# A gated transformer block and two sparse-attention layers: sliding-window attention between the projections, compression weights in a buffer of their own, later splits

## The chip, the cores and the metric

The kernel runs on one core of a Trainium2 chip. The metric is the device time in microseconds (us) of one launch. All tensors are float32 in memory.

## What is computed

The sequence has 256 tokens (T) and 1024 features (D, eight chunks of 128, C = 8). The first block, cut to what matters here:

```python
mod = silu(c) @ w_ada + b_ada                      # 6 x 1024 values, "modulation"
shift1, scale1, gate1, shift2, scale2, gate2 = split(mod, 6)
h = norm1(x) * (1 + scale1) + shift1
q_g, k_g, v_g, a_lr, r_g, q_s, k_s, v_s = split(h @ w_in)
log_a = log_sigmoid(a_lr @ w_gla_alpha + b) / 16
o_gla = rms_norm(gla_mixer(q_g, k_g, v_g, log_a)) * silu(r_g)  # 4 heads, chunks of 64 tokens
o_swa = rms_norm(swa_mixer(q_s, k_s, v_s, sinks))              # 8 heads of 64, softmax with a sink
x = x + gate1 * (concatenate([o_gla, o_swa]) @ w_out)
h2 = norm2(x) * (1 + scale2) + shift2
x = x + gate2 * peer_mixer(h2)                     # top 16 of 128 + 128 keys, 8 heads, 16384 experts
```

Then come a layer with DSA attention (an indexer picks 64 keys per query, 8 heads over a shared latent) and an MLP of 4096; the shared keys and values, of which two are compressed, `gelu(flat(blocks) @ w1) @ w2`, with a `w1` of 4096 x 256 for keys (w1k) and one for values (w1v); a layer with NSA attention and an MLP; and a last norm.

## The kernel before, in words

**Weights.** SyncE (SP) brings 488 blocks of 128 x 1024 floats (512 KB each) in one fixed order into `ring`, which has 4 places (RING). A load waits until the block four places ahead of it has been used (`slots_used`). Where a product needs more than one pass of precision, ScalarE (ACT) writes a rounded copy `ring_hi` (2 places, `split_high`, L368) and VectorE (DVE), or GpSimd (POOL) for `peer_q` and `peer_u`, writes the rest in place as `ring_lo` (`split_low`, L375). TensorE (PE) then does three matmuls for each 128 x 128 tile (`three`, L587 to L589): 24 for a block. The w_in projections use float32 matmuls straight from `ring`: `project` (L555) and `project_tokens` (L567), 16 records a block for `project`.

**Modulation.** The 48 rows of w_ada (512 KB each) are loaded by POOL's queue. The first 16 (shift1 and scale1) have places of their own; the other 32 pass through `aring`, 4 places, each load waiting in POOL's program (L444) until the row 4 ahead is used. `modulation` (L1638) multiplies and sums one row on DVE.

**Order of the first block.** (1) Modulation rows 0 to 5; the bias table waits for all six small loads (`small_loaded`, L1646); the norm of x is a sum over partitions with `ones` on PE (L577), a root on ACT, a reciprocal of 128 x 256 on DVE (L1649); then rows 6 to 15, each pair with one chunk of h. (2) 18 projections in the order q_g, k_g, r_g, q_s, k_s, v_g, v_s. Beside them DVE prepares the decays and rows 16 to 33. (3) The exponentials of the decays on ACT (L1288 to L1292), products on DVE (L1690 to L1695), then GLA on PE: scores (L755), transposes (L762), states (L771), inner part (L780), part between chunks (L788). (4) The norm of GLA: sums (L794, L795), roots, the reciprocal of 128 x 1024 (L1730), scaling (L1732), gate (L1736), splits of the result. (5) Sliding-window attention (`attend("swa")`): 16 units of one head and 128 queries, the first 8 with 128 keys, the others with 256; a unit has scores (L666), transposes (L675) and products (L702) on PE, bias, maximum and scaling on DVE, the exponential and copies on ACT. Rows 40 to 47 lie between its units. (6) Its norm. (7) w_out, 8 blocks; each yields one chunk of x, added by DVE (L1818). (8) The sum of squares of x (POOL adds chunks, L455, L458), norm 2, h2 chunk by chunk (L1804, L1810). (9) peer_q: 16 blocks, low parts by POOL; after each, DVE picks the best 16 keys (L1843 to L1853). (10) peer_u, 128 blocks.

**Memory.** `big` has 128 rows of 256 floats. In the first block it holds h, `aring`, silu(c) (`cs`, rows 37 to 40), projections and GLA's tensors. For the experts rows 40 to 127 must be set to one: POOL does this in three parts, `mid_lo` to `mid_hi` (rows 61 or 62 to 96) after GLA is done (L449), and the other two after the last split of the attention results (L451, L452). `ones_set` is awaited by DVE before the expert gates.

**Later layers.** Before `attend("dsa")` and `attend("nsa")`, ACT and DVE split the first block of a_o and the first two of b_o. In the compression w1k (8 blocks) and w1v (8 blocks) come through the ring one after the other (L1075 to L1077), 12 matmuls a block.

## Time and profile before

| | us |
|---|---|
| median of 3 runs (1765.46 to 1768.02) | 1766.5 |
| the profiled execution's own time | 1767.21 |
| its span, first to last instruction | 1765.6 |
| PE busy in the span | 1650.5 (93%) |
| DVE busy | 1078.7 (61%) |
| ACT busy | 855.1 (48%) |
| POOL busy | 487.9 (28%) |
| mean clock granted to TensorE | 0.951 of full |

The span leaves 1.6 us of the profiled execution outside it. Times of a stage below are counted from the span's start. PE's busy time says how long it had work, not how fast it did it: the granted clock of a stretch says that.

### The profile page before, as it was taken

How to read it: one execution, taken by the hardware profiler on the slowest of the kernel's cores; microseconds unless marked ns; L12 is line 12 of the kernel's file. 1: busy time of each engine (PE TensorE's matmuls, PEld its weight loads, DVE VectorE, ACT ScalarE, POOL GpSimd, SP SyncE). 2: the span in 40 equal slices, each digit the busy share in tenths (PEclk: the TensorE clock that was granted, in tenths of full speed). 3: DMA queues.
4: the chain of work that ended last, by engine and by line, in shares of the span. 5: the costliest groups of instructions: out<-in, count | busy, mean ns of one | idle time of the engine just before them, and what ended most of it. 6: DMA issues, size and time to landing. Idle time of an engine off the chain costs nothing.

```text
span 1765.6 us, 33664 instructions
## 1 busy us (share of the span) xinstructions
PE 1650.5 (93%) x11072; PEld 1492.8 (85%) x11072; DVE 1078.7 (61%) x2455; ACT 855.1 (48%) x1808; POOL 487.9 (28%) x465
## 2 busy tenths in 40 slices
PE   5975889998999999999999999889999998899998
PEld 2773689998999999987888887779999988789997
DVE  5536558953777771355555555866555665755555
ACT  3213445555454444555555554265555535654554
POOL 3110456986666668500000001320000000310000
PEclk8985699999999999999999999889999999999999
DMA  8861144554443445555555555215555456045554
GB/s 309 312 226 57 39 138 144 170 178 140 143 140 134 142 143 169 182 192 192 192 190 190 190 190 178 78 58 165 181 181 185 147 176 205 25 144 175 185 187 155
DMA packets 81329, 288.17 MB, mean 163 GB/s; under 512 B 10144, under 2 KB 11472, under 8 KB 81136
## 3 DMA queue, kind: packets, MB, share of 16 engines
q1 hardware_dynamic: 72448, 257.30, 44.6%
q0 software_dynamic: 7488, 26.87, 4.1%
q10 hardware_dynamic: 1328, 3.15, 0.5%
q8 instruction: 39, 0.64, 0.1%
q14 instruction: 26, 0.21, 0.0%
HBM read 284.66 MB, written 2.62 MB: 163 GB/s over the span
## 4 chain that ended last, share of the span: by engine, by line
PE 83%; DVE 8%; ACT 3%; issue 2%; DMA 2%; POOL 1%; SPq 0%; DVEq 0%; ACTq 0%; POOLq 0%
PE pu L587 12%; PE pu L588 12%; PE pu L589 12%; PE pacc L646 8%; PE pacc L644 8%; PE pacc L645 8%; PE pu L555 3%; PE pu L567 2%; PE pacc L587 2%; PE pacc L589 2%; PE pacc L588 2%; PE pacc L702 2%; PE pm L874 2%; PE pn L874 2%; DVE ring_lo L375 1%
## 5 line engine op out<-in xcount | busy, mean ns | idle before, releaser
L368 ACT ACTIVATE ring_hi<-ring 128x512 fp32r<-128x512 f32 x912 | 524.2, 622 | 546.7 <-PE pu L589 290.5
L375 DVE TENSOR_TENSOR ring_lo<-ring,ring_hi 128x512 fp32r<-128x512 f32 x624 | 407.4, 695 | 356.5 <-ACT ring_hi L368 356.1
L587 PE MATMUL pu<-Xh,ring_hi 128*128 128x256 f32 x1472 | 432.5, 294 | 21.6 <-DVE stats L1756 4.3
L588 PE MATMUL pu<-Xl,ring_hi 128*128 128x256 f32 x1472 | 420.1, 285 | 0.0
L589 PE MATMUL pu<-Xh,ring_lo 128*128 128x256 f32 x1472 | 420.0, 285 | 0.0
L375 POOL TENSOR_TENSOR ring_lo<-ring,ring_hi 128x512 fp32r<-128x512 f32 x288 | 370.3, 1307 | 131.4 <-ACT ring_hi L368 130.8
L587 PEld LDWEIGHTS pu<-Xh,ring_hi 128*128 128x128 f32 x1472 | 285.9, 194 | 28.8 <-issue 15.7
L588 PEld LDWEIGHTS pu<-Xl,ring_hi 128*128 128x128 f32 x1472 | 286.5, 195 | 0.2
L589 PEld LDWEIGHTS pu<-Xh,ring_lo 128*128 128x128 f32 x1472 | 285.8, 194 | 0.0
L644 PE MATMUL pacc<-ring_hi,vh 128*128 128x512 f32 x512 | 200.5, 392 | 0.0
L646 PE MATMUL pacc<-ring_lo,vh 128*128 128x512 f32 x512 | 200.5, 392 | 0.0
L645 PE MATMUL pacc<-ring_hi,vl 128*128 128x512 f32 x512 | 199.8, 390 | 0.0
L587 PE MATMUL pu<-X2h,ring_hi 128*128 128x256 f32 x512 | 146.3, 286 | 3.2 <-DVE big L2088 3.2
L589 PE MATMUL pu<-X2h,ring_lo 128*128 128x256 f32 x512 | 145.6, 284 | 0.0
L588 PE MATMUL pu<-X2l,ring_hi 128*128 128x256 f32 x512 | 145.6, 284 | 0.0
L644 PEld LDWEIGHTS pacc<-ring_hi,vh 128*128 128x128 f32 x512 | 96.0, 187 | 33.2 <-issue 5.6
L646 PEld LDWEIGHTS pacc<-ring_lo,vh 128*128 128x128 f32 x512 | 96.1, 188 | 21.0
L645 PEld LDWEIGHTS pacc<-ring_hi,vl 128*128 128x128 f32 x512 | 96.2, 188 | 16.0
L473 POOL DMA_DIRECT2D big<-bias_row x8 | 4.3, 549 | 363.1 <-DVE stats L1999 363.1
L587 PEld LDWEIGHTS pu<-X2h,ring_hi 128*128 128x128 f32 x512 | 99.0, 193 | 4.2 <-DVE big L2088 3.6
L588 PEld LDWEIGHTS pu<-X2l,ring_hi 128*128 128x128 f32 x512 | 98.9, 193 | 0.3
L589 PEld LDWEIGHTS pu<-X2h,ring_lo 128*128 128x128 f32 x512 | 99.0, 193 | 0.0
(390 smaller groups left out, 2653.1 us busy)
## 6 DMA issues: line engine op xcount, KB each, us to landing
ring<-in_weights SPq DMA_DIRECT2D x488, 512.0 KB, 3.3
big<-in_ada POOLq DMA_DIRECT2D x40, 512.0 KB, 6.7
bias_row<-big ACTq DMA_DIRECT2D x1, 1536.0 KB, 6.9
XT<-in_xT ACTq DMA_DIRECT2D x1, 1024.0 KB, 8.2
scr<-in_ada POOLq DMA_DIRECT2D x2, 512.0 KB, 12.3
tk<-in_ada POOLq DMA_DIRECT2D x2, 512.0 KB, 14.0
early_h<-in_ada POOLq DMA_DIRECT2D x2, 512.0 KB, 16.0
early_l<-in_ada POOLq DMA_DIRECT2D x2, 512.0 KB, 17.6
```

What stands on the lines that cost most here:

```text
L368: nc.scalar.activation(ring_hi[:, n % 2, half], ring[:, n % RING, half], ACT.Copy).then_inc(s["split_hi"], 1)
L375: api.tensor_tensor(ring_lo[:, n % RING, half], ring[:, n % RING, half], ring_hi[:, n % 2, half], ALU.subtract).then_inc(s[LOW[name][0]], 1)
L555: last = mm(entry(e), slot(n)[:, c * P:(c + 1) * P], rhs[:, c, :], start=(c == 0), stop=(c == C - 1))
L567: last = mm(entry(e)[:, tt * P:(tt + 1) * P], lhs[:, c, tt * P:(tt + 1) * P], slot(n)[:, c * P:(c + 1) * P], start=(c == 0), stop=(c == C ...
L587: mm(out, ring_hi[:, n % 2, w], xh, start=start, stop=False, skip_group_check=True)
L588: mm(out, ring_hi[:, n % 2, w], xl, start=False, stop=False, skip_group_check=True)
L589: return mm(out, ring_lo[:, n % RING, w], xh, start=False, stop=stop, skip_group_check=True)
L644: mm(out, xh[:, rows], ring_hi[:, n % 2, w], start=False, stop=False, skip_group_check=True)
L645: mm(out, xl[:, rows], ring_hi[:, n % 2, w], start=False, stop=False, skip_group_check=True)
L646: last = mm(out, xh[:, rows], ring_lo[:, n % RING, w], start=False, stop=False, skip_group_check=True)
L702: last = mm(out, v, p, start=(kind != "nsa" and k == 0 and UNITS[u][4]), stop=(k == len(pairs) - 1 and UNITS[u][5]), skip_group_check=(kin ...
L874: last = mm((pm, pn)[k % 2][:, i * P:(i + 1) * P], sq[:, j // 2, j % 2 * P:(j % 2 + 1) * P], scr[:, j * P:(j + 1) * P], start=True, stop=True)
```

## The change

First block. w_in is laid out as q_s, k_s, v_s, q_g, k_g, v_g, r_g. The 20 steps of the sliding-window attention are spread over the 12 projections from the seventh on (one or two after each, in the programs of PE and ACT), with scores in two PSUM banks (pm, pn) where they had four. ACT computes the decays' exponentials after the sixth projection; DVE's products for GLA and one modulation row are fillers between attention units. r_g is stored as it is, and its SiLU is taken once later. The three norms (n1, swa, gla) sum with tokens on partitions (a product with one column of ones), take the root and the reciprocal of a few columns, and spread them back by a matmul of a broadcast column with the identity; the scaling reads PSUM. w_out is laid out in 8 blocks of half the inputs and a quarter of the outputs: 4 blocks for the attention's half of the inputs, then 4 for GLA's. Each block adds into two chunks of x, so x is added to twice. Rows 40 to 43 of the modulation lie between these blocks, rows 44 to 47 behind h2. The bias table waits for its own two loads only. The first 16 rows of w_ada have six semaphores where they had eight (rows 8 to 11 and 12 to 15 are awaited as four). POOL's two last parts of setting ones are cut into 14 pieces, one behind each of the first 14 peer_q blocks; before the first peer_q split POOL waits until all 48 modulation rows are used. POOL's h2 sum leaves out one chunk more, which PE adds.

Later layers. w1k leaves the ring (480 blocks are left): POOL's queue loads its 4 MB into places of its own after the squares of the first MLP's input are summed, and its splits read from there. The first split of a_o, and the first two of b_o, are done between attention units.

The diff, cut:

```diff
-            for dst, src, sem in ((cols[:, :], cols_d, "cols_loaded"), (relb[0:NB, :], relb_d, "small_loaded"),
-                                  (oneh[0:NB, :], onehot_d, "small_loaded"), (walr, small_d[:, :, 0:16], "small_loaded"),
+            for dst, src, sem in ((cols[:, :], cols_d, "cols_loaded"), (relb[0:NB, :], relb_d, "relb_loaded"),
+                                  (oneh[0:NB, :], onehot_d, "relb_loaded"), (walr, small_d[:, :, 0:16], "small_loaded"),
...
             pool.wait_ge(s["gla_done"], 1)
             for k in range(mid_lo, mid_hi, 4):
                 step(nc.gpsimd.memset(big[:, k:min(k + 4, mid_hi), :], 1.0))
-            pool.wait_ge(s["x_split"], 2 * XSPLIT["w_out"] + 2)
-            step(nc.gpsimd.memset(big[:, GATED_FROM:mid_lo, :], 1.0))
-            nc.gpsimd.memset(big[:, mid_hi:NKEY, :], 1.0).then_inc(s["ones_set"], 1)
             pool.wait_ge(s["h2_sq"], 2)
             h2sum = R[:, T:2 * T]
             step(nc.gpsimd.tensor_tensor(h2sum, sq[:, 0, :], sq[:, 1, :], ALU.add))
-            for c in range(2, C - 1):
+            for c in range(2, C - 2):
                 pool.wait_ge(s["h2_sq"], c + 1)
                 last = nc.gpsimd.tensor_tensor(h2sum, h2sum, sq[:, c, :], ALU.add)
-                if c < C - 2:
+                if c < C - 3:
                     step(last)
             last.then_inc(s["h2_sum"], 1)
             pool.wait_ge(s["slots_used"], SLOT["peer_q"])
+            pool.wait_ge(s["x_split"], 2 * XSPLIT["w_out"] + 2)
+            pool.wait_ge(s["ada_used"], MOD)
+            parts = [(k, min(k + 4, hi)) for lo, hi in ((GATED_FROM, mid_lo), (mid_hi, NKEY)) for k in range(lo, hi, 4)]
             for i in range(2 * PH):
                 split_low(pool, nc.gpsimd, "peer_q", i)
+                for lo, hi in parts[i::2 * PH]:
+                    step(nc.gpsimd.memset(big[:, lo:hi, :], 1.0))
+            nc.gpsimd.memset(ones_flag, 1.0).then_inc(s["ones_set"], 1)
...
+            pool.wait_ge(s["slots_used"], SLOT["a_o"])
+            for k in range(8):
+                pool.dma_start(w1_raw[k], w1k_d[k, :, :]).then_inc(s["w1_full"], 16)
...
                 def scores(u):
-                    if u >= 4:
-                        pe.wait_ge(s["att_biased"], u - 3)
-                    mm(score_psum(u)[:, 0:keys_of(u)], query(u), keys(u), start=True, stop=True)\
+                    if u >= banks:
+                        pe.wait_ge(s["att_biased"], u + 1 - banks)
+                    mm(score_psum(u, banks)[:, 0:keys_of(u)], query(u), keys(u), start=True, stop=True)\
                         .then_inc(s["att_scored"], 1)
...
-            norm_sum("n1")
-            pe.wait_ge(s["small_loaded"], 16 * 6)
+            pe.wait_ge(s["squares"], SQUARED["n1"])
+            for tt in range(TT):
+                for c in range(C):
+                    last = mm(pn[:, tt:tt + 1], sq[:, c, tt * P:(tt + 1) * P], ones[:, 0:1], start=(c == 0), stop=(c == C - 1))
+            last.then_inc(s["sums"], 1)
+            pe.wait_ge(s["consts_made"], 1)
+            pe.wait_ge(s["inverses"], 1)
+            for tt in range(TT):
+                last = mm(pm[:, tt * P:(tt + 1) * P], over_columns(R[:, tt:tt + 1]), ident[:, :], start=True, stop=True)
+            last.then_inc(s["spreads"], 1)
+            pe.wait_ge(s["relb_loaded"], 16 * 2)
...
+            for i in range(18):
+                if i == 5 or 10 <= i < 14:
+                    project_tokens(SLOT["w_in"] + i, USE["w_in"] + i, HTf)
+                else:
+                    project(SLOT["w_in"] + i, USE["w_in"] + i, HTf)
...
+                if i == EARLY:
+                    pe.wait_ge(s["la_parts"], 1)
+                    pe.wait_ge(s["evacs"], USE["w_in"] + EARLY)
+                if i >= EARLY:
+                    for step in steps_after(i - EARLY, swa_steps):
+                        swa_step(SPAN["swa"][0] + step)
...
+            def out_slot(i):
+
+                n, e, x0 = SLOT["w_out"] + i, USE["w_out"] + i, i // 4 * 4
+                pe.wait_ge(s["evacs"], e - 1)
+                if i % 4 == 0:
+                    pe.wait_ge(s["x_split"], 2 * XSPLIT["w_out"] + i // 4 + 1)
+                for j in range(2):
+                    for c in range(4):
+                        if j == 0 and c % 2 == 0:
+                            split_ready("w_out", i, c // 2, None)
+                        last = three(pu[:, e % 2, j * T:(j + 1) * T], n, slice(c * T + j * P, c * T + (j + 1) * P),
+                                     Xh[:, x0 + c, :], Xl[:, x0 + c, :], c == 0, c == 3)
+                last.then_inc(s["slots_used"], 1)
...
+            out_slot(0)
             pe.wait_ge(s["squares"], SQUARED["gla"])
...
+            for h in range(GH):
+                for tt in range(TT):
+                    last = mm(paccf[:, h * TT + tt:h * TT + tt + 1], sq[:, h, tt * P:(tt + 1) * P], ones[:, 0:1], start=True, stop=True)
+            last.then_inc(s["sums"], 1)
+            out_slot(1)
+            pe.wait_ge(s["inverses"], 3)
+            for h in range(GH):
+                for tt in range(TT):
+                    col = 8 + h * TT + tt
+                    last = mm((pm, pn)[h // 2][:, (h % 2 * TT + tt) * P:(h % 2 * TT + tt + 1) * P], over_columns(R[:, col:col + 1]),
+                              ident[:, :], start=True, stop=True)
+            last.then_inc(s["spreads"], 1)
+            for i in range(2, 8):
+                out_slot(i)
...
-                    n = SLOT[name] + i
+                    n = SLOT["w1v"] + i
+                    high, low = ring_hi[:, n % 2, :], (ring_lo[:, n % RING, :] if kv else w1_lo[i][:, :])
...
+                        mm(out, xh, high[:, w], start=(i == 0 and l == 0), stop=False, skip_group_check=True)
+                        mm(out, xh, low[:, w], start=False, stop=False, skip_group_check=True)
+                        last = mm(out, xl, high[:, w], start=False, stop=(i == 7 and l == 3), skip_group_check=True)
+                    last.then_inc(s["slots_used" if kv else "w1_used"], 1)
...
+                if i == EARLY - 1:
+                    act.wait_ge(s["ex_ready"], 1)
...
+                    f(kp, kp, ACT.Exp, scale=inv).then_inc(s["ex_done"], 1)
+                    act.wait_ge(s["row_stored"], 16)
+                if i >= EARLY:
+                    for st in steps_after(i - EARLY, swa_steps):
+                        swa_step(SPAN["swa"][0] + st)
+            swa_step(SPAN["swa"][1] + 4)
+            act.wait_ge(s["att_out"], OUTNO[SPAN["swa"][1] - 1] + 1)
+            squares(os_, sq[:, 0:4, :])
...
+            split_high(act, "w_out", 0)
...
+            split_high(act, "w_out", 1)
+            act.wait_ge(s["evacs"], USE["w_in"] + 18)
+            f(rs, rs, ACT.Silu).then_inc(s["silu_done"], 1)
+            act.wait_ge(s["normed"], NORM["swa"])
+            x_high(os_, 0)
...
+            def dsa_between(i):
+
+                if i == 10:
+                    split_high(act, "a_o", 0)
+
+            attend("dsa", lambda u: (slice(0, P), oT[:, UNITS[u][2], UNITS[u][1] * P:(UNITS[u][1] + 1) * P]), dsa_between)
...
+            def w1k_high(i):
+
+                act.wait_ge(s["w1_full"], 16 * 8)
+                if i >= 2:
+                    act.wait_ge(s["w1_used"], i - 1)
+                for half in halves:
+                    f(ring_hi[:, (SLOT["w1v"] + i) % 2, half], w1_raw[i][:, half], ACT.Copy).then_inc(s["split_hi"], 1)
+
+            w1k_high(0)
...
+                if i == 10 or i == 12:
+                    split_high(act, "b_o", i // 2 - 5)
...
+            modulation(2 * C, 6)
...
+            def swa_filler(i):
+
+                modulation(2 * C + 6 + i, 1)
+                if 8 <= i < 8 + 3 + NSUB:
+                    gla_product(i - 8)
+
+            dve.wait_ge(s["consts_made"], 1)
+            dve.wait_ge(s["small_loaded"], 16 * 4)
+            attend("swa", swa_bias, filler=swa_filler)
+            modulation(2 * C + 23, 1)
...
+            dve.wait_ge(s["spreads"], 2)
+            for i in range(4):
+                last = v.scalar_tensor_tensor(os_[:, i, :], os_[:, i, :], column("swa_g", i), paccf[:, 0:T], ALU.mult, ALU.mult)
+            last.then_inc(s["normed"], 1)
+            split_low(dve, v, "w_out", 0)
...
-            step(v.reciprocal(Rg, Rg))
+            v.reciprocal(R[:, 8:8 + GH * TT], R[:, 8:8 + GH * TT]).then_inc(s["inverses"], 1)
+
+            def out_residual(i):
+
+                e = USE["w_out"] + i
+                dve.wait_ge(s["slots_used"], SLOT["w_out"] + i + 1)
+                for j in range(2):
+                    o = 2 * (i % 4) + j
+                    last = v.scalar_tensor_tensor(XT[:, o, :], pu[:, e % 2, j * T:(j + 1) * T], mod[:, 16 + o:17 + o], XT[:, o, :],
+                                                  ALU.mult, ALU.add)
+                last.then_inc(s["evacs"], 1)
+
+            out_residual(0)
+            modulation(2 * C + 25, 1)
+            dve.wait_ge(s["spreads"], 3)
...
+            dve.wait_ge(s["silu_done"], 1)
             v.tensor_tensor(og, og, rs, ALU.mult).then_inc(s["gla_done"], 1)
...
+            split_low(dve, v, "w_out", 2)
+            out_residual(1)
+            x_low("w_out", og, 1)
+            for i in range(2, C):
+                if i + 1 < C:
+                    split_low(dve, v, "w_out", i + 1)
+                out_residual(i)
+                if i < 4:
+                    modulation(2 * C + 24 + i, 1)
+            rest = 2 * C + 28
...
+            modulation(rest, MOD - rest)
+            dve.wait_ge(s["ada_used"], MOD)
+            step(v.tensor_tensor(mod[:, 40:48], mod[:, 40:48], cols[:, COL["b_ada"] + 40:COL["b_ada"] + 48], ALU.add))
...
+            def dsa_filler(i):
+
+                if i == 12:
+                    split_low(dve, v, "a_o", 0)
+
+            attend("dsa", dsa_bias, filler=dsa_filler)
...
+            def w1k_low(i):
+
+                for j, half in enumerate(halves):
+                    dve.wait_ge(s["split_hi"], 2 * (SPLIT["w1k"] + i) + j + 1)
+                    v.tensor_tensor(w1_lo[i][:, half], w1_raw[i][:, half], ring_hi[:, (SLOT["w1v"] + i) % 2, half], ALU.subtract)\
+                        .then_inc(s["split_lo"], 1)
+
...
+                elif i == 12 or i == 14:
+                    split_low(dve, v, "b_o", i // 2 - 6)
                 elif i == 23:
                     x_low("b_o", oT[:, 0:4, :], 0)
...
+    def halves_of(w):
+
+        return w.reshape(4, P, 4, T).transpose(2, 1, 0, 3).reshape(4, P, D)
...
+        tiles(np.concatenate([qs, ks, vs, qg, kg, vg, rg], axis=1)), halves_of(w_out[512:]), halves_of(w_out[:512]),
```

## Rows read from the trace of the kernel before

**Rows 1.** Busy time by stage: from:to, length, each engine's busy us (instructions), clock, DMA share, GB/s.

```profile
42.00:112.40 70.40, 67.65 (x373) 60.12 (x372) 28.75 (x46) 13.33 (x27) 9.52 (x18) 0.95 0.83 309
112.40:140.30 27.90, 17.49 (x212) 16.53 (x212) 13.69 (x27) 6.92 (x10) 3.17 (x6) 0.59 0.40 133
140.30:161.90 21.60, 5.01 (x12) 2.11 (x12) 14.15 (x15) 8.02 (x10) 0.00 (x0) 0.50 0.00 0
161.90:197.60 35.70, 32.83 (x96) 17.19 (x96) 29.05 (x98) 16.66 (x64) 10.34 (x13) 0.52 0.18 60
197.60:206.80 9.20, 3.49 (x9) 2.30 (x9) 3.58 (x6) 3.09 (x5) 0.00 (x0) 0.78 0.00 0
206.80:233.10 26.30, 26.30 (x194) 26.07 (x194) 12.54 (x21) 11.73 (x22) 16.14 (x8) 0.88 0.45 140
233.10:244.90 11.80, 6.34 (x26) 4.87 (x24) 9.21 (x20) 5.89 (x12) 4.93 (x4) 0.71 0.15 49
244.90:298.40 53.50, 51.11 (x427) 50.72 (x427) 38.04 (x223) 27.07 (x64) 36.93 (x30) 1.00 0.47 158
```

**Rows 2.** The waits of PE: who for whom, us in total, times, longest.

```profile
PE pm L755 <- DVE big L1695: 9.7, 1, 9.7
```

**Rows 3.** DVE's instructions in order of time at the start.

```profile
22.60 0.68 DVE L1647 COPY big<-big 32x1024 f32<-32x1024 f32 x1 [3.23 <-DMA sinks<-in_sinks]
23.21 1.73 DVE L1649 RECIPROCAL R<-R 128x256 f32<-128x256 f32 x1
```

**Rows 4.** One modulation row on DVE: min/median/max ns.

```profile
L1638 DVE CUSTOM_DVE_ANT_0 big<-big x40: 1204/1224/1409, 11.7 to 191.8; 128x1024 f32<-128x1024 f32 x40
```

**Rows 5.** The chain that ended last, in attention: 1.2 GHz at 184, 2.4 GHz at 1520.

```profile
184.84 0.62 PE pacc L675 x2
185.46 1.05 PE pacc L702 x4
186.50 1.15 PE pu L666 x2
...
1520.51 0.45 PE pacc L702 x4
1520.95 0.43 PE pn L666 x2
1521.39 0.11 PE pacc L675
```

**Rows 6.** Stages by clock: inside the projections, and the first of w_out.

```profile
52.50:59.40 6.90, 6.17 (x15) 4.96 (x16) 6.44 (x10) 0.86 (x3) 0.00 (x0) 0.51 0.37 117
59.40:112.40 53.00, 52.96 (x323) 48.59 (x321) 22.30 (x37) 7.03 (x17) 9.52 (x18) 1.00 0.88 327
206.80:213.00 6.20, 6.20 (x29) 6.20 (x30) 1.23 (x1) 1.65 (x3) 3.79 (x1) 0.50 0.00 0
```

**Rows 7.** POOL's groups, 160 to 235 us: busy us, mean ns, idle before.

```profile
L449 POOL MEMSET big<- 128x1024 f32 (+1 forms) x9 | 8.2, 915 | 0.5
L458 POOL TENSOR_TENSOR R<-R,sq 128x256 f32<-128x256 f32 x5 | 3.7, 739 | 7.2 <-ACT sq L1168 7.1
```

**Rows 8.** POOL's group in the peer_q stage, 244.9 to 296 us.

```profile
L375 POOL TENSOR_TENSOR ring_lo<-ring,ring_hi 128x512 fp32r<-128x512 f32 x28 | 35.6, 1293 | 17.9 <-ACT ring_hi L368 17.9
```

**Rows 9.** Groups in the compression, 1444 to 1476 us.

```profile
L375 DVE TENSOR_TENSOR ring_lo<-ring,ring_hi 128x512 fp32r<-128x512 f32 x30 | 19.3, 686 | 13.5 <-ACT ring_hi L368 13.2
L368 ACT ACTIVATE ring_hi<-ring 128x512 fp32r<-128x512 f32 x31 | 17.9, 623 | 15.0 <-DMA ring<-in_weights 9.3 <-PE pm L1077 4.8 <-PE pn L1077 0.8
```

**Rows 10.** DVE in order of time, before NSA's and DSA's first units.

```profile
1504.48 2.50 DVE L375 TENSOR_TENSOR ring_lo<-ring,ring_hi 128x512 fp32r<-128x512 f32 x4 [5.52 <-ACT ring_hi L368]
1506.90 0.28 DVE L2218 TENSOR_TENSOR big<-pm,big 128x128 f32<-128x128 f32 x1
...
1148.78 1.83 DVE L375 TENSOR_TENSOR ring_lo<-ring,ring_hi 128x512 fp32r<-128x512 f32 x2
1150.54 0.28 DVE L2071 TENSOR_TENSOR big<-pm,big 128x128 f32<-128x128 f32 x1
```

315 lines of the change are left out of this document (161 added, 154 removed).

## The prediction

> **What bounds the kernel now.** The page comes first: TensorE is busy for 93% of the span, so only stages with a slow or waiting PE can give much. The stage table shows where they are: from 112.4 to 206.8 us the granted clock is 0.50 to 0.59 of full, 0.78 in the last 9.2 us, and PE has 5.0 us of work in the 21.6 us of GLA's norm [rows 1]. The waits put one idle stretch of 9.7 us on DVE's last GLA product [rows 2]. The chain of waits then tells which engine each stage hangs on. The start hangs on DVE: 3.23 us for the last small load, then 0.6 and 1.7 us before the scaling [rows 3]. The projections hang on PE (67.7 of 70.4 us), attention on PE at 1.2 GHz (32.8 of 35.7), peer_q on PE (51.1 of 53.5) with POOL behind it at 36.9 [rows 1]. All times below are in the profiled execution, 1767.2 us, which is 0.7 above the median of 1766.5.
>
> **The start.** The bias table no longer waits for six loads (3.2 us of idle DVE), its copy (0.6) moves before row 0, and the reciprocal of 256 columns (1.7) becomes one of two: 5.5 us off DVE's line [rows 3]. Rows 4 and 5 are used after the reciprocal, when DVE would have waited. The new sum is 16 products with one column, 32 records. No such product is in the trace; bounds are a 128-column record at 2.4 GHz, 0.11 us, and at 1.2 GHz, 0.31 [rows 5], so 3.5 to 9.9 us against 5.3 us of room between the squares (11.7) and the end of row 3 (about 17). I take 0.13 each, nearer to the first, and 0.5 us of loss: minus 5.0 (minus 1 to minus 5.6). Projections then start at 37.1.
>
> **Attention between the projections.** Removed: 35.7 us [rows 1]. Added on PE: at 2.4 GHz a unit of 256 keys is 0.43 + 2 x 0.11 + 0.45 = 1.10 us, one of 128 keys half; at 1.2 GHz it is 0.62 + 1.05 + 1.15 = 2.82 [rows 5]. PE is kept busy, so I take the first: 8 x 1.10 + 8 x 0.55 = 13.2 us. Where two steps follow each other the product waits for ACT's copy, 0.3 us eight times, and the last unit's chain is open, 0.9: 16.5 together (13.2 to 32.8, today's busy time). DVE: today's 29.1 us less eight modulation rows of 1.3 (1.22 and a readout of 0.08) [rows 1, 4] leave 18.7; seventeen rows are 22.1 and GLA's products 4.4, so 45 us. They lie beside 11 projections of 3.5 us and 16.5, 55 us: covered, with 10 to spare. Projections end at 37.1 + 70.4 + 16.5 = 124.0, and the exponentials and products (9.7, rows 2) are under them.
>
> **GLA and w_out.** GLA's own steps are latencies in a stage of small matmuls at 0.59 [rows 1]: 18.2 us (27.9 less 9.7), kept as they are. Added: attention's norm, 8 one-column products (16 records, 2.0; 1.8 to 5.0) and two spreads (0.9): 145.1. Then ACT's queue decides: copies 1.2, one split 1.2, a table load and SiLU 2.3, the rounded copy of attention 1.1, and DVE's remainder 1.2, of which 3.3 us outlast the last GLA product: w_out starts at 148.4. A block is 24 matmuls, 5.1 us at 1.2 GHz (6.20 / 29 = 0.214 each) [rows 6] and 2.9 at full clock (51.1 / 427 = 0.12) [rows 1]. Block 0 at the low clock 5.1; GLA's sums 2.5; block 1 half and half 4.0; eight spreads 2.2; DVE then scales (1.7), gates (1.2) and splits block 2: PE waits 3.7; block 2 slow again 5.1; five blocks at 2.9 and small waits 14.9. Sum 37.5, against 26.3 now (30 to 43), end 185.9. GLA's norm (21.6) and attention's (9.2) are hidden or inside this sum. Against 233.1: minus 47.2.
>
> **To h2.** The last block adds and squares two chunks (plus 0.8). POOL is passed too: it issues the loads of rows 40 to 47 only when their places free, the last after row 43, which I put at 177 on DVE, so its first nine memsets (8.2 us) [rows 7], free now, end at 186, and five additions of 0.74 follow, 190, where PE wants the sum at 188: plus 2.4 (0 to 5). h2 is ready at 185.9 + 11.8 [rows 1] + 3.2 = 200.9, minus 44.0.
>
> **peer_q: the cost.** Today POOL has split the first two blocks before h2 is ready, and 16 blocks and the hand-over take 53.5 us from there [rows 1]. Now POOL waits for row 48, and DVE does rows 44 to 47 behind h2: 4 x 1.22 + 0.1 = 5.0 us. Nothing hides this, PE's first matmul waits for that split. Then POOL needs 35.6 / 14 = 2.54 us a block [rows 8] and 14 memsets of about 0.95 and a semaphore, 1.0 [rows 7]. PE's block is 3.3 us, POOL's now 3.54: POOL becomes the bound. 5.0 + 16 x 2.54 + 14 x 1.0 + PE's last half 1.5 + hand-over 3.7 = 64.8: plus 11.3 (5 if the memsets slip in, 14 if PE's clock falls in the longer idle). DVE's picks are not pushed: DVE idles there today until PE's first scores. Expert blocks start 32.7 us earlier, and nothing after them depends on more than that.
>
> **Compression.** ACT waits 9.3 us for ring loads there, DVE has 19.3 + 3 us of work in 32 us [rows 9]. With w1k at hand the ring refills behind it. A block is then held by the two places of ring_hi, a split half (0.62) and a remainder half (0.69) after block n-2, 1.5 us a block: I estimate 26.5 us, 5.0 to gain from 31.5 (2 to 8). The 4 MB are loaded in the first MLP, where the DMA engines are half free; 0.3 us for that (0 to 3).
>
> **Later splits.** NSA: DVE's first unit comes 2.5 us after the split begins [rows 10]; moved between units the splits cost 2 x 1.3 on DVE and 2 x 1.2 on ACT, both with some idle: minus 1.7 (minus 2.9 to plus 1). DSA: the split of 1.83 us before the first unit [rows 10] returns among units that run at DVE's pace: 0 (minus 1 to plus 1).
>
> In that row two halves take 0.92 us each, where four before NSA take 0.63 each: POOL adds its bias at the time [rows 10]. The Trainium skill (SBUF — State Buffer, Who interferes with whom) says that a DVE instruction with two SBUF inputs contends with a GpSimd instruction that reads SBUF. By that rule the moved a_o split stays at 1.83 and holds POOL's bias, and DSA's sum would be plus 0.7 rather than 0.
>
> **Sum.** -5.0 - 35.7 + 16.5 - 9.7 + 2.9 + 3.3 - 21.6 - 9.2 + 11.2 = -47.3 (47.2 by the clock times); +3.2; +11.3; -5.0; +0.3; -1.7 = -39.1. 1767.2 - 39.1 = 1728.1; less 0.7 gives 1727.4, forecast 1728.
>
> **Rivals.** (a) POOL's hand-over is free: the memsets fit PE's gaps and PE makes up the wait. Minus 13.7: 1714. For it: POOL idles 17.9 us in peer_q [rows 8]; against: that idle time is before its first split too, and the wait for row 48 stands in its program.
>
> (b) DVE sets the pace of the new order. If it gives a unit 1 us later than PE needs, 16 units are 16 us, and w_out's blocks with a modulation row between them (3.4 us of DVE against 2.9) add 4: 1748. For it: 45 of 55 us, in order, with a wait for ACT in each unit.
>
> (c) Slower than before: PE's clock. After the 2.7 us of waiting at 50.5, the next 6.9 us ran at 0.51 and held 15 records, one projection; at full clock 323 records, 160 of them in the five token blocks of 32 and 163 in blocks of 16, are 15.2 blocks in 53.0 us, 3.5 each [rows 6]. If waits for attention keep PE at 1.2 GHz, twelve projections cost 3.4 us more each, 41, and attention today's 32.8 in place of 16.5, 16: 1785. It passes the kernel before once eight of the twelve run so (8 x 4.8 = 38.4). Against: each projection is 3.5 us of unbroken work between the steps.
>
> The Trainium skill (TensorE: Matmul & The Clock Gate, HAM oscillation) warns that a loop which idles between short bursts of matmuls falls back to half clock each time. By that rule (c) is what happens; this trace shows it after one gap only.
>
> (d) The later layers' edits do nothing, as their waits are replaced by the next: plus 6.4, 1734, inside the forecast.
>
> **Chances.** The forecast with (d), 1720 to 1738: 0.57. (a), below 1720: 0.16. (b), 1738 to 1760: 0.21. (c) or any other loss: 0.05; no change 0.01. A measurement can tell 0.2% (3.5 us). Faster 0.94, same 0.01, slower 0.05. The range, 1712 to 1748, takes in (a) and most of (b); the unit costs alone (attention 13 to 33, w_out 30 to 43) span as much.
>
> **What would show it.** Projections from 37 to 124 us at a clock of 0.95 or more; no 128 x 1024 reciprocal; w_out in some 37 us with one wait of 3 to 4; POOL's first peer_q split after the 48th modulation row, and PE waiting for POOL in most peer_q blocks; ACT's wait for ring loads in the compression near 0. Projections at half clock, DVE as the releaser of PE between projections, or peer_q at 54 us would prove it wrong.

## The result, and the profile after

| | before | after |
|---|---|---|
| median of the runs taken together (4 each), us | 1766.3 | 1734.18 |
| lowest to highest, us | 1765.46 to 1768.02 | 1732.42 to 1737.05 |
| span of the profiled execution, us | 1765.6 | 1730.7 |
| mean clock granted to TensorE | 0.951 | 0.974 |

The two medians are 32.1 us apart. The ratio on record is 0.9833, with an interval of 0.9816 to 0.985, and 1.67% of 1766 us is 29.5 us. The kernel before was at the upper end of its scatter in this set: in the three later sets its medians were 1761.5, 1762.1 and 1764.4 us, and the changed kernel's ratio in two of them was 0.9834 and 0.9837, 29 us off. So the change is worth 29 to 32 us. The forecast was 39.1 off, 1728; its range of 1712 to 1748 holds 1734.2, and its case (d), the later layers' edits doing nothing, named 1734. The profiled execution is 1.8 us under the median; where that comes from is shown below.

Of the page of the changed kernel, the span in 40 slices: the granted clock of TensorE, in tenths of full. What is left of the low stretch is the 7s of the fourth slice (GLA and the start of w_out) and the fifth (h2 and the stretch behind it).

```profile
PEclk9997799999999999999999999899999999999999
```

The stages of the first block (windows of the changed kernel, from the first projection on: projections with attention, GLA, w_out, h2, the rows behind h2, peer_q), to be held against [rows 1]:

```profile
38.70:126.90 88.20, 85.48 (x469) 68.81 (x468) 56.64 (x145) 32.86 (x92) 12.68 (x24) 1.00 0.79 277
126.90:149.20 22.30, 19.52 (x242) 18.15 (x241) 7.76 (x18) 12.44 (x20) 0.00 (x0) 0.65 0.13 44
149.20:186.50 37.30, 30.93 (x224) 30.29 (x224) 24.39 (x49) 13.80 (x26) 12.46 (x16) 0.89 0.50 168
186.50:200.90 14.40, 2.90 (x6) 1.85 (x6) 8.83 (x18) 4.43 (x9) 1.44 (x2) 0.68 0.01 5
200.90:206.60 5.70, 0.01 (x1) 0.04 (x1) 4.42 (x10) 0.00 (x0) 1.37 (x2) 0.50 0.00 0
206.60:266.10 59.50, 57.07 (x449) 56.07 (x449) 38.19 (x224) 27.10 (x64) 52.59 (x48) 0.95 0.44 142
```

The reader sees 88.2 us for projections and attention, where it was 70.4 and 35.7, at a full clock (the last unit's last product still runs in the next window, to 128.6 us); w_out in 37.3 with GLA's norm under it, where norm, attention's norm and w_out were 21.6, 9.2 and 26.3; and then a new stretch of 5.7 us in which PE does nothing.

What the attention costs between the projections is read from the chain that ended last. A unit of 128 keys, then one of 256, each between two projections (scores L696, transposes L705, products L732):

```profile
85.72 0.42 PE pm L696 x2
86.13 0.26 PE pacc L705
86.39 0.36 PE pacc L732 x2
...
104.20 0.63 PE pm L696 x2
104.82 0.37 PE pacc L705 x2
105.19 0.58 PE pacc L732 x4
```

That is 1.04 and 1.58 us, and 8 of each are 21.0 us. No wait lies between them; PE waits once, 0.3 us, before the last product.

The waits of 185 to 275 us name the cause of the stretch of 5.7 us, and a smaller one ahead of it:

```profile
PE pu L615 <- POOL ring_lo L397: 17.8, 2, 15.5
POOL ring_lo L397 <- DVE mod L1762: 17.1, 1, 17.1
...
PE pn L907 <- POOL R L477: 4.4, 1, 4.4
```

PE waits 15.5 us for POOL's first peer_q remainder, POOL 17.1 for DVE's modulation rows (L1762), and PE 4.4 for POOL's sum (L477). The chain of waits shows rows 44 to 47, the first split, and how peer_q then runs at POOL's pace, a split (L397) and a fill (L488) in turn:

```profile
200.42 1.14 DVE big L1762
...
203.85 1.14 DVE big L1762
205.23 1.27 POOL ring_lo L397
206.59 0.55 PE pu L615
...
239.57 0.96 POOL big L488
240.60 1.81 POOL ring_lo L397 x2
...
243.09 0.96 POOL big L488
```

From one fill to the next it is 3.52 us (243.09 - 239.57); in [rows 1] a block took 3.3, the hand-over included (53.5 / 16). The first expert block starts at 266.1 us, 32.3 earlier than before, and from there on both kernels do the same for 1465 us. The other 2.6 us of the span's 34.9 come in four places: 1.0 lost up to the compression, 1.8 gained from its start to the compressed scores, 0.4 in NSA, and 1.4 at the start of the last MLP.

That last one isn't the change's. The same instructions of that start, before and then after (windows of 3 us, the first from 3 us behind the same reciprocal's start):

```profile
1580.00:1583.00 3.00, 2.32 (x14) 2.32 (x15) 1.69 (x4) 1.76 (x4) 0.00 (x0) 0.79 0.57 184
1583.00:1586.00 3.00, 3.00 (x20) 3.00 (x19) 0.90 (x3) 1.37 (x4) 0.00 (x0) 0.64 0.01 3
```

```profile
1546.50:1549.50 3.00, 2.36 (x19) 2.36 (x20) 1.69 (x4) 1.77 (x4) 0.00 (x0) 1.00 0.52 176
1549.50:1552.50 3.00, 3.00 (x27) 2.98 (x26) 2.02 (x5) 1.77 (x4) 0.00 (x0) 1.00 0.31 67
```

PE has the same work behind the same idle time; its granted clock was 0.79 and 0.64 in the one and 1.00 in the other.

### The profile page after: what moved, and what is told of

Read it like the earlier page. It is cut to its first block, busy times and chain, and to the rows that moved or that the text cites. A ratio compares the mean times of both kernels' runs of the same rounds, so it can differ in the third digit from the quotient of the medians.

```text
span 1730.7 us, 33796 instructions
## 1 busy us (share of the span) xinstructions
PE 1639.6 (95%) x11134; PEld 1490.6 (86%) x11134; DVE 1067.3 (62%) x2463; ACT 851.8 (49%) x1806; POOL 492.4 (28%) x485
## 4 chain that ended last, share of the span: by engine, by line
PE 82%; DVE 7%; POOL 5%; issue 3%; ACT 3%; DMA 1%; DVEq 0%; ACTq 0%; POOLq 0%; SPq 0%
PE pu L615 12%; PE pu L616 11%; PE pu L617 11%; PE pacc L672 8%; PE pacc L674 8%; PE pacc L673 8%; POOL ring_lo L397 3%; PE pu L583 3%; PE pu L595 2%; PE pacc L615 2%; PE pacc L617 2%; PE pacc L616 2%; PE pn L960 2%; PE pm L960 2%; PE pacc L732 1%
## 5 line engine op out<-in xcount | busy, mean ns | idle before, releaser
L390 ACT ACTIVATE ring_hi<-ring 128x512 fp32r<-128x512 f32 x896 | 515.0, 622 | 545.8 <-PE pu L617 304.9
L397 DVE TENSOR_TENSOR ring_lo<-ring,ring_hi 128x512 fp32r<-128x512 f32 x608 | 395.9, 693 | 329.0 <-ACT ring_hi L390 328.8
L397 POOL TENSOR_TENSOR ring_lo<-ring,ring_hi 128x512 fp32r<-128x512 f32 x288 | 370.2, 1307 | 131.9 <-ACT ring_hi L390 113.6
L615 PEld LDWEIGHTS pu<-X2h,ring_hi 128*128 128x128 f32 x512 | 98.3, 192 | 4.2 <-DVE big L2254 3.6
L616 PEld LDWEIGHTS pu<-X2l,ring_hi 128*128 128x128 f32 x512 | 98.3, 192 | 0.3
L617 PEld LDWEIGHTS pu<-X2h,ring_lo 128*128 128x128 f32 x512 | 98.3, 192 | 0.0
```

What stands on the lines that cost most here:

```text
L390: nc.scalar.activation(ring_hi[:, n % 2, half], ring[:, n % RING, half], ACT.Copy).then_inc(s["split_hi"], 1)
L397: api.tensor_tensor(ring_lo[:, n % RING, half], ring[:, n % RING, half], ring_hi[:, n % 2, half], ALU.subtract).then_inc(s[LOW[name][0]], 1)
L615: mm(out, ring_hi[:, n % 2, w], xh, start=start, stop=False, skip_group_check=True)
L616: mm(out, ring_hi[:, n % 2, w], xl, start=False, stop=False, skip_group_check=True)
L617: return mm(out, ring_lo[:, n % RING, w], xh, start=False, stop=stop, skip_group_check=True)
```

## How far one execution differs from the next

Twelve more kernels were run, the changed one twice among them. Each profile gives a length for the stages that all of them share. Stages: start of the projections; the last remainder of h2 begins; from there to the lists' transposes on PE (peer_q and the first experts); the compression's two halves, first to last block; from its end (hidden units turned) over NSA to the last MLP's reciprocal; from there to the end. All in us.

| kernel | projections | h2 | to the lists | compression | NSA and b_o | last MLP |
|---|---|---|---|---|---|---|
| before | 42.0 | 244.3 | 179.1 | 32.9 | 97.7 | 188.6 |
| changed | 38.6 | 199.9 | 191.2 | 32.0 | 97.4 | 187.2 |
| changed, again | 38.5 | 204.0 | 191.9 | 32.3 | 98.1 | 188.7 |
| changed, third | 38.4 | 203.8 | 190.2 | 31.6 | 97.1 | 187.2 |
| first two splits early | 38.5 | 202.4 | 186.2 | 30.9 | 98.9 | 187.2 |
| fills on DVE | 38.5 | 201.5 | 184.8 | 32.1 | 98.9 | 187.2 |
| middle fills later | 38.4 | 197.9 | 190.8 | 30.8 | 98.9 | 187.2 |
| attention behind | 38.5 | 216.5 | 189.2 | 30.8 | 98.9 | 187.2 |
| splits early | 38.5 | 202.2 | 190.2 | 32.3 | 98.8 | 187.2 |
| w1k through the ring | 38.4 | 203.8 | 190.2 | 31.3 | 97.2 | 187.2 |
| first block alone | 38.6 | 199.9 | 191.2 | 32.2 | 98.3 | 187.3 |
| halves interleaved | 38.6 | 199.9 | 191.2 | 30.4 | 97.0 | 187.3 |
| fills spread | 38.5 | 201.2 | 182.5 | 31.1 | 98.9 | 187.2 |
| all together | 38.3 | 202.4 | 183.0 | 28.2 | 97.0 | 188.6 |

With one program h2 came at 199.9, 204.0 and 203.8 us. The 4 us lie in two places. After PE's wait of 2.7 us for ACT, which ends at 49.8 us, the clock was 1.00 in the profile first shown and 0.88 in the second, over 14 us: the attention's last product ends 1.6 us later. And GLA's scores ran at 0.95 to 1.00 in the one, while in the other the clock fell to 0.50 among them: from their start to the transposes 4.5 us and 6.3 us (windows, then rows of PE by line, first execution, then second):

```profile
46.00:60.00 14.00, 11.28 (x52) 9.64 (x52) 10.49 (x17) 4.64 (x8) 1.06 (x2) 1.00 0.66 217
...
130.00:134.00 4.00, 4.00 (x100) 3.97 (x98) 0.76 (x2) 0.31 (x2) 0.00 (x0) 0.95 0.08 32
```

```profile
46.00:60.00 14.00, 11.29 (x45) 9.31 (x44) 10.60 (x17) 4.53 (x8) 1.06 (x2) 0.88 0.58 180
...
133.00:138.00 5.00, 5.00 (x67) 4.96 (x65) 0.76 (x2) 0.50 (x1) 0.00 (x0) 0.50 0.00 0
```

```profile
L824 PE MATMUL pm<-big 64*64 64x16 f32 x64 | 2.8, 209 | 0.0
```

```profile
L824 PE MATMUL pm<-big 64*64 64x16 f32 x64 | 3.8, 238 | 0.0
```

In the first of these pairs the last column but two is the granted clock, 1.00 and 0.95 against 0.88 and 0.50. So the first profile of the changed kernel was one of the better executions of its first block. It reaches the lists at 391.1 us, 32.3 earlier than the one profile of the kernel before (423.4); the other two reach them at 395.9 and 394.0, 27.5 and 29.4 earlier. The forecast, which came within 0.5 us of the first profile at 266 us, was 3 to 5 us too good for the others. The second is also the slowest of its set of five (1732.2 to 1741.6 us, itself 1741.6).

For what follows: a stage with an idle stretch in it repeats to 1 or 2 us only, and the stage lengths tell more than the totals, whose ratios have intervals of 0.17 to 0.25 per cent, 3 to 4 us, to either side. The next four kernels had no run of the changed kernel beside them, so their totals are compared through their ratios to the kernel before, with the 0.9834 of the second set.

## Experiments on the first block

**All attention steps behind the last projection.**

```diff
 def steps_after(k, total):
-    return range(k * total // BESIDE, (k + 1) * total // BESIDE)
+    return range(total if k == BESIDE - 1 else 0)
...
-            attend("swa", swa_bias, filler=swa_filler)
+            for i in range(17):
+                modulation(2 * C + 6 + i, 1)
+            for i in range(3 + NSUB):
+                gla_product(i)
+            attend("swa", swa_bias)
```

> The changed kernel, with all twenty steps of the attention behind the last projection, in their new form (two banks of scores, DVE's modulation rows and GLA products ahead of them, so that DVE has only the attention's own 18.7 us). Theory: the attention is cheap between the projections because they fill PE's time while ACT and DVE work on a unit, and keep its clock at full; by itself it is a chain over four engines in which PE idles and its clock falls to 0.5, as in the kernel before: 30 to 36 us in place of the 15 to 16 that it adds now, so 15 to 20 us slower than the changed kernel, 1749 to 1754. Rival 1: what made it dear was only the low clock it inherited, and right behind the projections it starts at the full one: 16 units at some 1.2 us, under 5 us slower, 1739. Rival 2: DVE sets its pace when spread (a row of 1.3 us in every unit), then this order is no slower: 1734 or less.

Measured: 1747.28 us, ratio 0.9916 (0.9898 to 0.9934); the changed kernel's 0.9834 of the same time is 14.4 less. The windows behind the last projection:

```profile
112.00:120.00 8.00, 8.00 (x25) 4.21 (x25) 5.77 (x29) 5.07 (x23) 0.00 (x0) 0.61 0.00 0
120.00:128.00 8.00, 8.00 (x22) 3.60 (x21) 4.74 (x18) 3.40 (x13) 0.00 (x0) 0.50 0.01 3
128.00:136.00 8.00, 8.00 (x24) 4.22 (x22) 3.57 (x15) 3.36 (x12) 0.00 (x0) 0.50 0.00 0
```

The attention begins at 108.8 us at the full clock, but the 8 us from 112 are at 0.61 already and the next 16 at 0.50. PE counts as busy all the while, with 22 to 25 matmuls in 8 us. A unit of 256 keys costs 2.82 us on the chain (1.15, 0.62 and 1.05), as in [rows 5], against 1.58 between the projections. Rival 1 falls by this, rival 2 by the time.

This profile also gives the price of both orders. Here the projections alone take 70.3 us (38.5 to 108.8) and the attention alone 33.9 (to 142.7). Their clock was 0.76 from 46 to 60 us, before PE's two programs differ. By my estimate that costs 0.24 of 14 us, 3.4: without it the projections are 66.9. In the changed kernel both together end at 128.6, 89.9 us after their start at 38.7, and its clock was 1.00 there: so the attention costs 23.0 us between the projections. The second execution gives the same (91.6 us, of which 1.7 are its clock of 0.88). The interleaving itself saves 33.9 - 23.0 = 10.9 us; the rest of the 14.4, as far as the profiles show it, is the clock that GLA inherits and the one ahead of the attention. The new form in its old place saves 1.8 (35.7 - 33.9). The theory's 15 to 20 was a little high.

**POOL splits the first two peer_q blocks ahead of its wait.**

```diff
             pool.wait_ge(s["slots_used"], SLOT["peer_q"])
+            split_low(pool, nc.gpsimd, "peer_q", 0)
+            split_low(pool, nc.gpsimd, "peer_q", 1)
             pool.wait_ge(s["x_split"], 2 * XSPLIT["w_out"] + 2)
             pool.wait_ge(s["ada_used"], MOD)
...
-                split_low(pool, nc.gpsimd, "peer_q", i)
+                if i >= 2:
+                    split_low(pool, nc.gpsimd, "peer_q", i)
```

> The changed kernel, with POOL splitting the first two peer_q blocks before it waits for the 48th modulation row (the two fills that stood behind them come after that wait). Theory: the wait of 5.0 us for rows 44 to 47 stands on the path, and after it POOL is the bound at 3.54 us a block. Then PE starts its first block at about 201 us in place of 206.6, POOL has two blocks (5.1 us) done when row 47 ends at 205, and the first expert block comes at 205 + 14 x 2.54 + 14 x 1.0 + 5 = 260 in place of 266.1: 6 us off, about 1728. Rival: the pace of the sixteen blocks is set by something else than POOL (DVE's picks, PE at its low clock after the wait), and the earlier start turns into waits inside peer_q: under 1 us off, 1734.

Measured: 1730.65 us, ratio 0.9822 (0.9804 to 0.984). From h2 to the lists 186.2 us, where the nine kernels with an unchanged hand-over have 189.2 to 191.9, 190.7 in the mean: 4.5 off, where the theory of the hand-over said 6. The total moved by 2.1 (0.0012 of 1762), which its interval neither tells from nothing nor from 4.5.

**The fills on DVE**, behind its last modulation row:

```diff
-            pool.wait_ge(s["x_split"], 2 * XSPLIT["w_out"] + 2)
-            pool.wait_ge(s["ada_used"], MOD)
...
-                for lo, hi in parts[i::2 * PH]:
-                    step(nc.gpsimd.memset(big[:, lo:hi, :], 1.0))
...
+            dve.wait_ge(s["x_split"], 2 * XSPLIT["w_out"] + 2)
+            for lo, hi in [(k, min(k + 4, hi)) for lo, hi in ((GATED_FROM, mid_lo), (mid_hi, NKEY)) for k in range(lo, hi, 4)]:
+                v.memset(big[:, lo:hi, :], 1.0)
```

> The changed kernel, with the 14 fills taken from between POOL's peer_q splits and done by DVE right behind the modulation rows, where DVE waits some 15 us for PE's first key scores; POOL then needs no wait for row 48 either. Theory: both terms of the hand-over go, the wait (5.0 us) and POOL's pace: a block costs PE's 3.2 to 3.3 us, and the first expert block comes at 201 + 16 x 3.25 + 3.7 = 257 in place of 266.1: 9 us off, 1725. Rival: DVE is late with its picks (the fills are some 14 us of DVE) and the hand-over to the lists moves, or POOL's splits were not the bound: 0 to 5 us off.

Measured: 1731.26 us, ratio 0.9824 (0.9806 to 0.9841). The last key scores come 52.4 us after h2, where they came 63.6, 62.8 and 62.8 after it (58.6 with the first two splits early): 10.4 off or more, so both terms of the hand-over were real. But to the lists it is 184.8, only 5.9 under the mean, and the total moved by 1.8 us, where the theory said 9 and the rival 0 to 5. The rival was right about the rest: DVE began its picks at 224 us, and ACT, which must copy key scores before it can split the next block, waited for them. The waits of 185 to 275 us, POOL for ACT and ACT for DVE:

```profile
POOL ring_lo L397 <- ACT ring_hi L390: 29.9, 16, 10.2
...
ACT scr L1250 <- DVE tk L2013: 11.7, 8, 2.8
```

**POOL's middle fills behind its sum for h2** (the loop over mid_lo to mid_hi moved below the h2_sum semaphore).

> The changed kernel, with POOL's nine fills of the middle behind its sum for h2 instead of ahead of it. Theory: PE's wait of 4.4 us for that sum goes, all of DVE's work behind it moves up, and POOL has 188 to 205 us free for the fills: 4 us off, 1730. Rival: POOL's sum then waits for ACT's squares of the last chunks, which end only some 2 us before PE wants it, and the fills run into the first splits: 0 to 1.5 us off.

Measured: 1730.82 us, ratio 0.9824 (0.9805 to 0.9842). From the start of w_out to the last matmul of the sum 37.6 us, where it is 41.3, 41.5 and 41.6: 3.7 to 4.0 off, and PE no longer waits for the sum. The theory holds in the stage; the total moved by 1.8 us, which can't be told from nothing or from 4.

**The fills spread.** All fills behind the last peer_q split, ten of them among the expert blocks:

```diff
-            pool.wait_ge(s["x_split"], 2 * XSPLIT["w_out"] + 2)
-            pool.wait_ge(s["ada_used"], MOD)
...
+            pool.wait_ge(s["x_split"], 2 * XSPLIT["w_out"] + 2)
+            pool.wait_ge(s["ada_used"], MOD)
...
+            for q in range(4):
+                fill(q)
+            for k in range(3 * BODY):
+                split_low(pool, nc.gpsimd, "peer_u", k)
+                if k % 2:
+                    fill(4 + k // 2)
             nc.gpsimd.memset(ones_flag, 1.0).then_inc(s["ones_set"], 1)
-            with pool.Fori(0, NKEY // BODY) as g:
+            with pool.Fori(3, NKEY // BODY) as g:
```

and the middle fills behind the sum.

> The changed kernel, with POOL's middle fills behind its sum for h2, and the other 14 fills behind its last peer_q split: four at once, where POOL waits 5 us for the hand-over to the expert blocks, and ten behind every second of the first peer_u splits; POOL splits peer_q with no wait for row 48. Theory: the three measured gains add without DVE's delay, since DVE does no fills: 3.7 us from the sum, 5.0 from the wait, and 3 to 6 from POOL's pace: 12 to 15 us before the lists, 1719 to 1722. Rival: DVE's picks (first key scores to the lists) become what the lists wait for, as with the fills on DVE, where 4.8 us were given back: 7 to 9 us, 1725.

Measured: 1727.93 us, ratio 0.9798 (0.9779 to 0.9817), beside the changed kernel's 1735.07 and 0.9837: 7.1 us off (6.9 by the ratios), the fastest version here. The size is the rival's, the reason isn't. The stages: w_out's start to the end of the sum 37.3 us, 4.1 off; h2 to the last key scores 52.5, 10.5 off; from there to the lists 130.0, where the changed kernel has 127.6, 129.1 and 127.4, so the ten fills cost some 2 (PE waits 5.7 us for POOL's splits there, 3.9 in the changed kernel); and, foreseen by neither, h2 itself, which comes 13.2 us after the sum in place of 9.4. POOL, free of its wait, splits peer_q while DVE scales h2 (the timeline of POOL, then of DVE):

```profile
194.39 5.60 POOL L397 TENSOR_TENSOR ring_lo<-ring,ring_hi 128x512 fp32r<-128x512 f32 x4
203.21 4.18 POOL L397 TENSOR_TENSOR ring_lo<-ring,ring_hi 128x512 fp32r<-128x512 f32 x2 [3.22 <-ACT ring_hi L390]
```

```profile
194.14 0.47 DVE L1985 SCALAR_TENSOR_TENSOR Xl<-big,mod,Xh 128x256 fp32r<-128x256 f32 x1
194.54 1.48 DVE L1979 SCALAR_TENSOR_TENSOR big<-XT,gain,R 128x256 f32<-128x256 f32 x1
...
198.78 1.49 DVE L1985 SCALAR_TENSOR_TENSOR Xl<-big,mod,Xh 128x256 fp32r<-128x256 f32 x1
200.19 0.47 DVE L1979 SCALAR_TENSOR_TENSOR big<-XT,gain,R 128x256 f32<-128x256 f32 x1
```

A scaling that takes 0.47 us takes 1.48 beside POOL's split, four of them in a row: 4.0 us more, on the path, and the next one, behind POOL's four halves, takes 0.47 again. That makes 4.1 + 10.5 - 3.8 - 2 = 8.8, and 7.1 were measured. Splitting only one block before h2 is ready, or having the middle fills stand there as they do in the changed kernel, might avoid this; it wasn't tried.

## Experiments on the later layers

**The later layers' edits undone, both** (first block alone; the hunks are those of the two experiments below).

> The changed kernel without both of its edits to the later layers: early splits of a_o and b_o, and the key half of the compression through the ring. Forecast of the prediction: the later edits are worth 5.0 - 0.3 + 1.7 = 6.4 us, so 6.4 slower than the changed kernel, 1740. Rival, after the first nine runs: the compression gives 1.7, the late splits nothing that can be told: 1.5 to 2.5 us slower, 1736.

Measured: 1735.19 us, ratio 0.9841 (0.9823 to 0.9859), beside 1735.07 and 0.9837. The two edits are worth 0.1 us by the medians and 0.7 by the ratios, and the two sets of five runs lie over each other (1733.6 to 1735.8, and 1732.5 to 1735.5). The forecast's 6.4 is out, and the rival's 1.5 to 2.5 is not borne out either.

**The splits of a_o and b_o early again.**

```diff
+            split_high(act, "a_o", 0)
-                if i == 10:
-                    split_high(act, "a_o", 0)
...
+            split_low(dve, v, "a_o", 0)
-            attend("dsa", dsa_bias, filler=dsa_filler)
+            attend("dsa", dsa_bias)
```

and the same for the two of b_o.

> The changed kernel, with the first split of a_o ahead of the DSA attention and the first two of b_o ahead of the NSA attention again. Forecast of the prediction: 1.7 us slower than the changed kernel (NSA 1.7, DSA 0). Rival, from the two traces: the attention starts 1.2 us (DSA) and 2.7 us (NSA) earlier with the late splits but ends only 0.2 earlier or 0.2 later (DSA) and 0.4 earlier (NSA), because the splits come back between units where DVE and POOL set the pace: 0 to 0.6 us slower, no difference that can be told.

Measured: 1735.78 us, ratio 0.9839 (0.9819 to 0.986), beside the changed kernel's 1733.41 and 0.9834 (0.9809 to 0.9858). No difference that can be told. NSA's stage is 98.8 and 98.3 us with early splits (97.7 in the kernel before) and 97.0 to 98.9 with late ones. In DSA, from the index step that ends the choice of keys to the split of the output, it is 27.5 us with the late split and 27.1 (here) and 27.3 (before) without, though the attention begins 1.2 us sooner. What DVE pays for the split, early and then late (rows of DVE over the DSA attention):

```profile
L1733 DVE TENSOR_SCALAR big<-big,stats 128x256 f32<-128x256 f32 x8 | 2.8, 355 | 0.3
...
L397 DVE TENSOR_TENSOR ring_lo<-ring,ring_hi 128x512 fp32r<-128x512 f32 x2 | 1.8, 951 | 0.0
```

```profile
L1739 DVE TENSOR_SCALAR big<-big,stats 128x256 f32<-128x256 f32 x8 | 3.3, 409 | 0.3
...
L397 DVE TENSOR_TENSOR ring_lo<-ring,ring_hi 128x512 fp32r<-128x512 f32 x2 | 1.3, 679 | 0.0
```

The prediction had weighed that the moved split stays at 0.92 a half and holds POOL's bias. It falls to 0.68: it starts at 1131.88 us, and POOL's last bias of this attention, from 1131.07 to 1131.80, is over. DVE's scaling just ahead of it meets that bias instead and takes 0.79 us where its neighbours take 0.35.

**w1k through the ring again.**

```diff
-            pool.wait_ge(s["slots_used"], SLOT["a_o"])
-            for k in range(8):
-                pool.dma_start(w1_raw[k], w1k_d[k, :, :]).then_inc(s["w1_full"], 16)
...
-                    high, low = ring_hi[:, n % 2, :], (ring_lo[:, n % RING, :] if kv else w1_lo[i][:, :])
+                    high, low = ring_hi[:, n % 2, :], ring_lo[:, n % RING, :]
```

> The changed kernel, with the eight blocks of the compression's key half loaded through the ring again, in place of eight buffers of their own. Forecast of the prediction: 5.0 - 0.3 = 4.7 us slower than the changed kernel. Rival, from the two traces: the wait for the ring did not go but moved to the value half (DMA 4.8 us on the chain there), and the stage gained 1.8 us: 1.5 to 2 us slower.

Measured: 1737.42 us, ratio 0.985 (0.9829 to 0.987): 4.0 above the changed kernel by medians, 2.8 by ratios, with intervals that overlap. The stage says less: its sixteen blocks take 31.3 us through the ring here and 32.2 in the kernel with the first block alone, and 30.8 to 32.3 with buffers of their own, 31.5 in the mean of nine (the two interleaved ones left out). The granted clock moves these lengths by 1 us or more: where it fell twice in the stage, 32.2 through the ring stands against 32.0 to 32.3, where it fell once, 31.3 against 30.8 and 30.9. In the changed kernel one ring load is on the chain of the stage, in this one there are two:

```profile
1435.32 4.77 DMA ring<-in_weights
```

```profile
1426.02 4.37 DMA ring<-in_weights
...
1436.31 4.32 DMA ring<-in_weights
```

and yet its blocks take at most 0.5 us longer. So the total's 3 to 4 us have no place in the stage that they should come from, and the other kernel with w1k in the ring (first block alone) hasn't them. The profiled run is the fastest of its five (1734.8 to 1739.4 us), so it can't show what the others lose; the changed kernel's own runs reach from 1732.2 to 1741.6. What the 3 to 4 us are stays open.

**The halves interleaved.**

```diff
+ORD = [(0, i) for i in range(4)] + [(1, i) for i in range(4)] + [(0, i) for i in range(4, 8)] + [(1, i) for i in range(4, 8)]
...
-            for kv in range(2):
+            for m, (kv, i) in enumerate(ORD):
```

with the splits of ACT and DVE in the same order.

> The changed kernel, with the sixteen compression blocks in the order keys 0 to 3, values 0 to 3, keys 4 to 7, values 4 to 7, in place of all keys and then all values. The four ring places are full of values when the stage begins, and no load starts until the first of them is used; now that comes four blocks earlier, and the next four values have four blocks of keys to arrive behind. Theory: what kept the missing 3 us of the compression term is the load of the fifth value block (4.8 us on the chain), so 3 us faster than the changed kernel or a little more. Rival: ACT's and DVE's split cadence holds the stage anyway: under 0.7 us.

Measured: 1733.2 us, ratio 0.9827 (0.9808 to 0.9846), beside 1733.41 and 0.9834. The load is gone from the chain, and the sixteen blocks take 30.4 us. The clock fell twice in this stage, to 0.58 and 0.77 over 4 us each; kernels with the old order in which it did so too (to 0.67 and 0.69 in the changed one, 0.59 and 0.76 with the fills on DVE, 0.57 and 0.78 with the splits early) took 32.0, 32.1 and 32.3, and those in which it fell once 30.8 and 30.9. So 4.8 us of load were taken off the chain, and 1.6 came back at a like clock. That is a fair part of the theory's 3 and more than the rival's 0.7, in one profile each; the totals don't show it. Both have a part: the load, and the cadence of the splits. What is left on the waits, ACT for PE and PE for DVE's remainder:

```profile
ACT ring_hi L1256 <- PE pn L1165: 5.3, 4, 3.2
DVE ring_lo L2335 <- ACT ring_hi L1256: 4.2, 4, 1.4
PE pn L1163 <- DVE ring_lo L2335: 3.5, 2, 2.3
```

**All together**: the fills spread, the halves interleaved, and both Gelus behind the last split.

> The kernel with the fills spread, and besides the interleaved halves of the compression with both Gelus behind the last split, so that the table load (1.3 us) does not stand between two splits. Theory: 1.5 us from the order of the blocks and 1.3 from the Gelus on top, 2.8 faster than the fills alone. Rival: the split cadence of ACT and DVE holds the stage as it did with the order alone: under 1 us.

Measured: 1728.65 us, ratio 0.9804 (0.9784 to 0.9824), beside 1727.93 and 0.9798 without them. The sixteen blocks take 28.2 us, 2.9 less than with the fills alone, but the Gelus now stand behind them, and from the gates to the hidden units turned it is 36.8 against 37.9: 1.1 gained, the last MLP's start lost 1.4 with the clock as in the kernel before, and the total shows nothing.

The changed kernel was run twice more beside these:

> The changed kernel itself, beside the three that follow, so that they are compared with it on the same chip. Its ratio to the kernel before was 0.983; the same is expected. Two profiled executions of it also show how far the stages differ from one execution to the next: if the 1.4 us that the last MLP gained are a matter of TensorE's clock in one execution, they come and go between the two.

> The changed kernel once more, as the base of the three that follow; ratio 0.983 to the kernel before. A third profiled execution: the stages from h2 to the lists should agree with the other two to 0.3 us, and those with short stops of TensorE (GLA, the first MLP's end, the compression) should again differ by 1 to 3 us with the granted clock.

Measured: 1733.41 us, ratio 0.9834 (0.9809 to 0.9858), and 1735.07, ratio 0.9837 (0.9817 to 0.9856). The last MLP's 1.4 us were there in one (187.2), and not in the other (188.7), as expected; "0.3 us from h2 to the lists" was too tight, it was 190.2 to 191.9.

## Why the prediction was right, and where it was not

By its own steps, against the first profile of the changed kernel:

- The start: minus 5.0 forecast, minus 3.3 measured (42.0 to 38.7). The 32 one-column records took 7.0 us, 0.22 each, not 0.13, where 5.3 us of room were counted on.
- Attention between projections, 16.5: the mechanism is right, the clock, and this term is the most mis-sized one of the first block. It measured 23.0 us. The prediction took its unit prices (1.10 and 0.55) from the NSA attention's rows at 1520 us [rows 5]; this attention's units are 1.58 and 1.04, and the 0.3 us waits between steps didn't occur. The window's 88.2 - 70.4 = 17.8 us looks like a hit by luck: the kernel before had lost 3.4 us of its 70.4 to a clock of 0.51 over 6.9 us [rows 6], which isn't there in this execution, and the last product (1.7 us) falls behind the window. DVE was covered, rival (b) is out; the clock held, rival (c) is out in this order and is what happens in the other.
- GLA and w_out: start 148.4 forecast, 149.2 measured. That is luck too. The attention ended 4.6 us later than forecast (128.6 for 124.0), and from there to w_out it was 20.6 us, 24.4 forecast: the scores took 4.5 us to the transposes, where they took 7.8 in the kernel before at half clock, and 6.3 in the second execution. The attention's norm sum was 3.2 us (2.0 forecast). w_out 37.5 forecast, 37.3 measured, with the one wait of 3.7 for DVE.
- To h2: 200.9 forecast, the remainders end at 200.4. PE's wait for POOL's sum was 4.4 us, the forecast's estimate 2.4, inside its bounds of 0 to 5.
- The hand-over, plus 11.3: h2 to the first expert block 65.7 us against 64.8 forecast. Right in size and in both parts, since each could be taken away: 4.4 us of 63.0 with the wait for row 48, a further 6.2 with the fills. Rival (a) is out.
- Compression, minus 5.0: this is the step that failed; the runs find 0 to 1 us. The sentence "a block is then held by the two places of ring_hi ..., 1.5 us a block: I estimate 26.5 us, 5.0 to gain from 31.5" took ACT's 9.3 us of waiting for the ring for time on the path. Without the ring the key half takes 15.6 to 17.4 us for its eight blocks, 2.0 to 2.2 each, as it does with the ring (15.2 and 17.0): so most of ACT's waits lay beside other work. What else makes up the 2 us, the runs don't separate; DVE's remainder of the input (2.3 us) stands on the chain of this stage, and the clock falls in it. And the first four value blocks wait in the ring for their turn, so that the fifth is only asked for when the first is used.
- NSA, minus 1.7: not found. 0.4 in the two first traces, nothing beyond the scatter in all of them.
- DSA at 0 and w1k's loads at plus 0.3: no stage there moved by more than the scatter, so neither is contradicted, and 0.3 can't be told.

First block: 32.7 forecast, 32.3 by the first pair of profiles, 27.5 and 29.4 by the other two; later layers: 6.4 forecast, 0.1 to 0.7 found by undoing both edits. Measured 1734.2 is 6.2 above 1728: case (d), by its number and by its reason. The forecast of the first block is good in its total because errors of 2 to 7 us in its terms have different signs.
